# Second seven-product unit of the gate and up chunks moved from the sixth to the eighth plain slot

## The chip, the cores and the metric

The kernel runs on one NeuronCore of one Trainium2 chip. The metric is the device time of one execution in microseconds. An execution of the kernel before was also taken with the hardware profiler; the rows below come from that one.

## What is computed

The reference is one layer of a streaming encoder for 256 tokens of width 2048, all in float32. The change touches only its first and its last block, the two feed-forward networks (FFN), which have the same form:

```python
def _swiglu_ffn(x, norm_g, w_gate, w_up, w_down):
    h = _rmsnorm(x, norm_g)
    return (jax.nn.silu(h @ w_gate) * (h @ w_up)) @ w_down

h = h + 0.5 * _swiglu_ffn(h, ffn1_norm[l], ffn1_w_gate[l], ffn1_w_up[l], ffn1_w_down[l])
...
h = h + 0.5 * _swiglu_ffn(h, ffn2_norm[l], ffn2_w_gate[l], ffn2_w_up[l], ffn2_w_down[l])
```

`w_gate` and `w_up` are 2048 x 5632, `w_down` is 5632 x 2048. Between the two FFNs stand two recurrent branches, their merge and an attention over a memory; they are the same in both kernels.

## The kernel before, in words

**Split operands.** Every matrix product is made from three TensorE matmuls with 512 columns each: both operands are split into a high and a low part (`whi`, `wlo` for weights, `xhi`, `xlo` for activations), and the kernel adds high x high, low activation x high weight, high activation x low weight (lines 794 to 796). ScalarE makes the high part of a weight slot by a copy with rounding (line 371, function `split_hi`; line 847 inside a unit). VectorE makes the low part by subtraction (line 376, `split_lo`; line 865 inside a unit).

**Slots.** Weights come in raw slots of two 128 x 512 blocks (512 KB), loaded by the SP queue into a ring of four (`raw`); the split parts have a ring of four as well (`whi`, `wlo`). ScalarE may write slot n when TensorE has finished slot n - 4 (`slot_used`), VectorE when ScalarE has written it (`whi_ready`), TensorE reads it when VectorE has (`wlo_ready`), and SP loads a raw slot anew when VectorE has read it (`raw_free`).

**Gate and up chunks.** An FFN has 11 chunks of 512 hidden columns. Chunk 0 is made in the plain way. In chunks 1 to 10 (`SEVEN`) gate and up are made as a pair: six of the eight slots of gate and the same six of up are plain slots, t = 0 to 5 for gate and t = 6 to 11 for up (`na` is 6), with 12 matmuls each. The remaining slots 6 and 7 of both are two **units**: a unit takes one raw slot of gate and one of up and makes the eight block products of two token halves, two k blocks and gate or up from seven, with sums of weight blocks (VectorE, lines 872, 876 and 881, into `tw`), sums of activations (`xshi`, `xslo`) and sums of results. It fills four slots of the ring, `w` to `w + 3`, with 6, 6, 3 and 6 matmuls. Four of its results go into banks of their own (`pa`, `pb`), which both units of a chunk share. Where the units stand among the plain slots is written out in `GU_AFTER`: behind t = 1 and behind t = 5.

**What follows the second unit.** ScalarE copies one bank out (line 891, `copy_first`, at t = 6). VectorE combines the banks (lines 898 and 899, `combine`, at t = 8; line 902, `combine_last`, at t = 9) and adds the gate banks in (line 1063, at t = 9). Line 1063 releases the gate banks, for which TensorE waits at the start of the next chunk, and also frees ScalarE to apply the activation (line 982, at t = 10). The up half is subtracted, and gate times up is formed, in the next chunk, in the middle of its first unit (`gated`, lines 1025 and 1031, called between the second and third step of `unit_dve`). TensorE waits for that at the third slot of the unit.

**The hidden tile's way.** The result `hid` is turned by VectorE at t = 3 (line 705), written to DRAM and read back by the POOL queue (lines 668 and 678), then split at t = 9 by ScalarE (line 759, `hidden_hi`) and at t = 11 by VectorE (line 763, `hidden_lo`), which waits at line 1065 for the activation of its own chunk.

**What sets the order.** Each engine has its own loop over the same plain slots (`ffn_load` for SP, `ffn_pe`, `ffn_act`, `ffn_dve`), and what is to be done beside a slot is tied to its number t. The engines take their instructions in this order; semaphores alone tie them together. The chunk's last slot on one engine is followed at once by the next chunk's first.

Of the kernel before, what the change touches and what calls it, by code (L numbers as in the profile page):

```python
# [19 lines left out]
KT = D // P  # L20
# [5 lines left out]
NFC = F // CW  # L26
# [95 lines left out]


SEVEN = range(1, NFC)
GU_UNITS, GU_AFTER = (6, 7), (1, 5)
DN_UNITS = {"f1": ((0, 1, 2, 3, 4, 5), (2, 3, 4, 5)), "f2": ((0, 1, 2, 3, 4, 5), (0, 1, 2, 3, 4, 5))}
DN_AFTER = {"f1": ((7, 11, 15, 19, 23, 27), (5, 9, 13, 17)), "f2": ((7, 11, 15, 19, 23, 27), (3, 7, 11, 15, 19, 23))}
DN_FORMS = {5: 0, 9: 1, 17: 2}
# [3 lines left out]
def plan():  # L132

    prods, turns, nats = {}, {}, {}
    moved = {}
    state = dict(p=0, slot=0, raw=0, t=0, s=0, n=0, d=0, freed=[0, 0])
    raw_of, freed_by = {}, {}
    last = [None, None]

    def plain_slot():  # L140
        w, r = state["slot"], state["raw"]
        raw_of[w], freed_by[r] = r, w
        state["slot"] += 1
        state["raw"] += 1
        return w, r

    def unit_slots():

        w, r = state["slot"], state["raw"]
        freed_by[r], freed_by[r + 1] = w + 2, w + 2  # L150
        state["slot"] += UW
        state["raw"] += 2
        return w, r

    def pair_slots(a, b, units, after):

        js = [j for j in range(a["ns"]) if j not in units]
        pair = dict(a=a, b=b, after=after, plain=[], units=[], na=len(js))
        for t, (pr, j) in enumerate([(a, j) for j in js] + [(b, j) for j in js]):
            pair["plain"].append((pr, j, *plain_slot()))  # L160
            if t < len(js):
                a["done"] = state["slot"]
            if t in after:
                pair["units"].append((units[after.index(t)], *unit_slots()))
                a["done"] = state["slot"]
        b["done"] = state["slot"]
        a["pair"] = b["pair"] = pair

    def products(phase, n, nk, ups=None, seven=None):
        out = []  # L170
        for c in range(n):
            k = nk[c % len(nk)]
            par = state["p"] % 2
            if ups is not None and c % 2 == 1:
                released = ("nat_ready", ups + c // 2 + 1)
            else:
                state["freed"][par] += 1
                released = (("pair_free0", "pair_free1")[par], state["freed"][par])
            pr = dict(par=par, slot=state["slot"], raw=state["raw"], ns=k // SK, free=last[par], released=released)
            out.append(pr)  # L180
            last[par] = released
            state["p"] += 1
            if seven is not None and seven(c // 2) is not None:
                if c % 2 == 1:
                    pair_slots(out[-2], pr, *seven(c // 2))
                continue
            for j in range(pr["ns"]):
                plain_slot()
            pr["done"] = state["slot"]
        prods[phase] = out  # L190

    def turned(phase, n, split=True, nat=True, by_pe=None):
        by_pe = n if by_pe is None else by_pe
        turns[phase], nats[phase], moved[phase] = (state["t"] - (n - by_pe), state["s"]), state["n"], state["d"]
        state["t"] += by_pe
        state["d"] += n - by_pe
        if split:
            state["s"] += n
        if nat:
            state["n"] += n  # L200

    def ffn(tag):
        turned(tag + "norm", NDC, nat=False, by_pe=NDC if tag == "f1" else 1)
        turned(tag + "act", NFC, by_pe=0)
        products(tag + "gu", 2 * NFC, [KT], ups=nats[tag + "act"], seven=lambda i: (GU_UNITS, GU_AFTER) if i in SEVEN else None)
        products(tag + "dn", NDC, [FT], seven=lambda q: (DN_UNITS[tag][q], DN_AFTER[tag][q]))

    ffn("f1")
    turned("mixnorm", NDC, nat=False, by_pe=1)
    products("aux", 1, [KT])  # L210
    for hf in range(HALVES):
        products(f"gdn{hf}", 3, [KT])
    for hf in range(HALVES):
        products(f"rw{hf}", 3, [KT])
    products("gates", 2 * NDC, [KT])
    products("lift", 2 * NDC, [8])
    turned("merged", NDC, by_pe=1)
    products("out", NDC, [KT])
    turned("memnorm", NDC, by_pe=0)
    products("mkv", 2 * NDC, [KT])  # L220
    turned("mk", NDC, False, nat=False, by_pe=0)
    turned("qnorm", NDC, by_pe=0)
    products("mq", NDC, [KT])
    turned("mq", NDC, False)
    products("mo", NDC, [KT])
    ffn("f2")
    return prods, turns, nats, moved, raw_of, freed_by

# [27 lines left out]
def build(nc, A):  # L256

    prods, turns, nats, moved, raw_of, freed_by = plan()
    SUMS, ACTS, BANKS = count_marks()
    with ExitStack() as ctx:  # L260
        sems = {}

        def sem(name):
            if name not in sems:
                sems[name] = ctx.enter_context(nc.semaphore(name))
            return sems[name]
# [638 lines left out]
        def ffn_pe(pe, tag):  # L905
            gu, dn = prods[tag + "gu"], prods[tag + "dn"]
# [10 lines left out]
            for i in SEVEN:  # L917
                pair = gu[2 * i]["pair"]
                wait_pair(pe, pair["a"]["free"])
                for t in range(len(pair["plain"])):  # L920
                    plain_pe(pe, pair, t, (xhi, xlo))
                    if t in GU_AFTER:
                        n = GU_AFTER.index(t)
                        if n == 0:
                            pe.wait_ge(sem("banks_free"), BANKS[tag, "x"] if i == SEVEN[0] else BANKS[tag, "gu", i - 1])
                        unit_pe(pe, pair, n, (xhi, xlo), (xshi, xslo), n)
            pe.wait_ge(x_ready, s0 + NFC - 1)
            for q in range(NDC // 2):
                pair, after = dn[2 * q]["pair"], DN_AFTER[tag][q]
# [3 lines left out]
                for t in range(whole_slots):  # L933
# [3 lines left out]
                    if t in after:  # L937
                        n = after.index(t)
# [10 lines left out]
        def ffn_act(act, tag, then=None, gain=None):  # L949

            gu, dn = prods[tag + "gu"], prods[tag + "dn"]
# [15 lines left out]
            for i in SEVEN:  # L967
                pair = gu[2 * i]["pair"]
                gate = pair["a"]
                for t, (_, _, w, _) in enumerate(pair["plain"]):  # L970
                    split_hi(act, w, 0)
                    if t in GU_AFTER:
                        unit_act(act, pair, GU_AFTER.index(t), (tag, "gu", i))
                    if t == pair["na"]:
                        act.wait_ge(nat_ready, n0 + i)
                        copy_first(act, pair, cb[:, 0, :])
                    if t == pair["na"] + 3:
                        hidden_hi(act, tag, i - 1, hhi[:, 4 * i - 4:4 * i, :])
                    if t == pair["na"] + 4:
                        act.wait_ge(sem(gate["released"][0]), gate["released"][1])  # L980
                        for tt in range(TT):
                            op = nc.scalar.activation(gs[:, tt, :], cb[:, tt, :], ACT.Silu, scale=rstd[:, tt:tt + 1])
                        op.then_inc(sem("acts_ready"), 1)
            for q in range(NDC // 2):
                pair, after = dn[2 * q]["pair"], DN_AFTER[tag][q]
# [30 lines left out]
        def ffn_dve(dve, tag, then=None, gain=None):  # L1016
            gu, dn = prods[tag + "gu"], prods[tag + "dn"]
# [29 lines left out]
            for i in SEVEN:  # L1047
                pair = gu[2 * i]["pair"]
                gate = pair["a"]
                for t, (_, _, w, _) in enumerate(pair["plain"]):  # L1050
                    split_lo(dve, w, 0)
                    if t == 3:
                        nat_turn(dve, None, nats[tag + "act"] + i - 1)
                    if t in GU_AFTER:
                        n = GU_AFTER.index(t)
                        if n == 0 and i == SEVEN[0]:
                            dve.wait_ge(sem("banks_free"), BANKS[tag, "x"])
                        unit_dve(dve, pair, n, (tag, "gu", i), between=(lambda: gated(i - 1)) if n == 0 else None)
                    if t == pair["na"] + 2:
                        combine(dve, pair, cb, (tag, "gu", i))  # L1060
                    if t == pair["na"] + 3:
                        combine_last(dve, cb, (tag, "gu", i))
                        v.tensor_tensor(cb[:, 0:2, :], pair_of(gate), cb[:, 0:2, :], ALU.add).then_inc(sem(gate["released"][0]), 1)
                    if t == pair["na"] + 5:
                        dve.wait_ge(sem("acts_ready"), ACTS[tag, "gu", i, "gate"])
                        hidden_lo(dve, tag, i - 1, hhi[:, 4 * i - 4:4 * i, :], hlo[:, 4 * i - 4:4 * i, :])
            for q in range(NDC // 2):
                pair, after = dn[2 * q]["pair"], DN_AFTER[tag][q]
# [1923 lines left out]
```

## Time and profile before

| what | value |
|---|---|
| median of 3 runs | 2614.71 us (2613.63 to 2615.78) |
| the profiled execution, its own time | 2605.74 us |
| its span, first to last instruction | 2604.0 us |
| granted TensorE clock, mean | 0.998 |
| TensorE matmul busy | 2563.2 us (98%) |
| VectorE busy | 1954.3 us (75%) |
| ScalarE busy | 1341.0 us (51%) |

The span is what the rows below add up in; 1.74 us lie around it. A time in a row of the timeline is counted from the span's start. A matmul is shown with 0.39 us, but a new one starts every 0.2267 us, since they are pipelined: what counts is the distance of the starts. "[1.22 <-ACT whi L371]" behind a row says that the engine stood idle for 1.22 us before it and that ScalarE's line 371 ended this. In a wait row, "26.3, 10, 3.1" is the total in us, the number of times and the longest.

### The profile page before, as it was taken

Reading aid. Unit: us, or ns where it says so; the run is one execution under the profiler, and the core shown is the slowest. Engines: PE = TensorE matmul, PEld = TensorE weight load, DVE = VectorE, ACT = ScalarE, POOL = GpSimd, SP = SyncE. Lnnn points to the kernel's source line nnn. Section 1 sums busy time; section 2 is a strip of 40 time slices with the busy share of each in tenths; the row PEclk is TensorE's granted clock in tenths of the full one; section 3 lists DMA queues with packets and bytes.
Section 4 is the critical chain, followed back from the end, with each engine's and each line's share of the span. In section 5 each row is a group of like instructions: output and inputs, shape, how many; then the busy total and the mean of one; then the engine's idle time right before and its main releaser. Section 6 shows DMA issues by size and latency. Waiting matters only on the chain.

```text
span 2604.0 us, 34220 instructions
## 1 busy us (share of the span) xinstructions
PE 2563.2 (98%) x13659; PEld 2104.6 (81%) x13659; DVE 1954.3 (75%) x2311; ACT 1341.0 (51%) x1568; POOL 189.3 (7%) x346
## 2 busy tenths in 40 slices
PE   8999999998999999999999999999999999999998
PEld 7888888886788787878788888888888888888786
DVE  6888888876766796958666666555668888888876
ACT  5555555554456365546455444433455555555554
POOL 2000000000000011010001112000100000000000
PEclk9999999999999999999999999999999999999999
DMA  6767677666666675556488779644767676777554
GB/s 213 235 215 237 212 233 223 213 209 201 212 207 183 193 209 178 170 172 186 140 277 272 237 244 289 201 156 136 235 188 233 223 228 219 226 227 232 189 201 170
DMA packets 278576, 548.21 MB, mean 211 GB/s; under 512 B 25020, under 2 KB 35424, under 8 KB 278032
## 3 DMA queue, kind: packets, MB, share of 16 engines
q1 hardware_dynamic: 253904, 478.60, 58.3%
q0 software_dynamic: 24192, 66.89, 8.7%
q8 instruction: 107, 1.75, 0.3%
q10 hardware_dynamic: 320, 0.53, 0.1%
q14 instruction: 53, 0.43, 0.1%
HBM read 508.15 MB, written 37.77 MB: 210 GB/s over the span
## 4 chain that ended last, share of the span: by engine, by line
PE 68%; issue 18%; DVE 8%; DMA 3%; ACT 2%; POOL 1%; SPq 0%; DVEq 0%; ACTq 0%; POOLq 0%
PE pp L415 11%; PE pp L416 11%; PE pp L417 11%; PE pp L794 8%; PE pp L796 8%; PE pp L795 8%; DMA hid_dram<-hid_t 2%; DVE wlo L376 2%; POOL xq L678 1%; ACT whi L371 1%; PE pb L796 1%; PE pb L795 1%; PE pb L794 1%; PE pa L794 1%; PE pa L796 1%
## 5 line engine op out<-in xcount | busy, mean ns | idle before, releaser
L376 DVE TENSOR_TENSOR wlo<-raw,whi 128x1024 fp32r<-128x1024 f32 (+1 forms) x764 | 918.6, 1215 | 354.3 <-ACT whi L371 335.8
L371 ACT ACTIVATE whi<-raw 128x1024 fp32r<-128x1024 f32 (+1 forms) x764 | 798.7, 1054 | 620.6 <-PE pp L417 426.2
L794 PE MATMUL pp<-whi,xhi 128*128 128x512 f32 x1040 | 404.6, 389 | 0.0
L795 PE MATMUL pp<-whi,xlo 128*128 128x512 f32 x1040 | 404.6, 389 | 0.0
L796 PE MATMUL pp<-wlo,xhi 128*128 128x512 f32 x1040 | 404.6, 389 | 0.0
L415 PE MATMUL pp<-whi,xhi 128*128 128x512 f32 (+1 forms) x928 | 370.3, 399 | 0.7 <-DVE xlo L533 0.7
L417 PE MATMUL pp<-wlo,xhi 128*128 128x512 f32 (+1 forms) x928 | 359.3, 387 | 0.0
L416 PE MATMUL pp<-whi,xlo 128*128 128x512 f32 (+1 forms) x928 | 359.2, 387 | 0.0
L847 ACT ACTIVATE whi<-tw 128x1024 fp32r<-128x1024 f32 x124 | 131.6, 1062 | 272.4 <-PE pp L796 122.9
L794 PE MATMUL pp<-whi,hhi 128*128 128x512 f32 x572 | 224.6, 393 | 14.4 <-DVE wlo L376 14.4
L795 PEld LDWEIGHTS pp<-whi,xlo 128*128 128x128 f32 x1040 | 195.2, 188 | 40.7
L796 PEld LDWEIGHTS pp<-wlo,xhi 128*128 128x128 f32 x1040 | 195.2, 188 | 40.5
L794 PEld LDWEIGHTS pp<-whi,xhi 128*128 128x128 f32 x1040 | 195.2, 188 | 40.3
L795 PE MATMUL pp<-whi,hlo 128*128 128x512 f32 x572 | 223.3, 390 | 0.0
L796 PE MATMUL pp<-wlo,hhi 128*128 128x512 f32 x572 | 223.1, 390 | 0.0
L415 PEld LDWEIGHTS pp<-whi,xhi 128*128 128x128 f32 x928 | 174.4, 188 | 43.2 <-issue 7.2
L417 PEld LDWEIGHTS pp<-wlo,xhi 128*128 128x128 f32 x928 | 174.3, 188 | 36.1
L865 DVE TENSOR_TENSOR wlo<-tw,whi 128x1024 fp32r<-128x1024 f32 x124 | 151.5, 1222 | 67.6 <-ACT whi L847 67.6
L416 PEld LDWEIGHTS pp<-whi,xlo 128*128 128x128 f32 x928 | 174.6, 188 | 32.3
L847 ACT ACTIVATE whi<-raw 128x1024 fp32r<-128x1024 f32 x124 | 104.7, 845 | 121.9 <-PE pp L796 89.4
L794 PEld LDWEIGHTS pp<-whi,hhi 128*128 128x128 f32 x572 | 107.7, 188 | 40.9 <-DVE wlo L376 18.6
L872 DVE TENSOR_TENSOR tw<-raw 128x1024 f32<-128x1024 f32 x62 | 75.9, 1225 | 79.2 <-DMA raw<-in_ffn_w_up 48.4
(528 smaller groups left out, 3670.3 us busy)
## 6 DMA issues: line engine op xcount, KB each, us to landing
raw<-in_ffn_w_gate SPq DMA_DIRECT2D x176, 512.0 KB, 4.4
raw<-in_ffn_w_up SPq DMA_DIRECT2D x176, 512.0 KB, 4.6
raw<-in_ffn_w_down SPq DMA_DIRECT2D x176, 512.0 KB, 4.6
raw<-in_w_in SPq DMA_DIRECT2D x144, 512.0 KB, 4.4
hid_dram<-hid_t POOLq DMA_DIRECT2D x43, 512.0 KB, 4.9
xq<-hid_dram POOLq DMA_DIRECT2D x156, 128.0 KB, 4.0
raw<-in_w_lift SPq DMA_DIRECT2D x32, 512.0 KB, 5.5
raw<-in_w_out SPq DMA_DIRECT2D x32, 512.0 KB, 5.3
```

Source lines behind the costliest of these rows:

```text
L371: nc.scalar.activation(whi[:, s, :, 0:width], raw[:, r % RING, :, 0:width], ACT.Copy).then_inc(whi_ready, 1)
L376: nc.vector.tensor_tensor(wlo[:, s, :, 0:width], raw[:, r % RING, :, 0:width], whi[:, s, :, 0:width].bitcast(F32), ALU.subtract).then_inc( ...
L415: nc.tensor.matmul(out, a_hi[:, k0 + k, tok], w_hi, start=first, stop=False)
L416: nc.tensor.matmul(out, a_lo[:, k0 + k, tok], w_hi, start=False, stop=False)
L417: mm = nc.tensor.matmul(out, a_hi[:, k0 + k, tok], w_lo, start=False, stop=final)
L678: nc.gpsimd.dma_start(landing[rows, :, :, :].rearrange("p q m j -> p q (m j)"), scratch.rearrange("(q i) e -> i q e", q=4)[:, :, 256 * b:2 ...
L794: nc.tensor.matmul(out, a_hi, whi[:, s, block, :], start=start, stop=False)
L795: nc.tensor.matmul(out, a_lo, whi[:, s, block, :], start=False, stop=False)
L796: return nc.tensor.matmul(out, a_hi, wlo[:, s, block, :], start=False, stop=stop)
L847: nc.scalar.activation(dst, src, ACT.Copy).then_inc(whi_ready, 1)
L865: v.tensor_tensor(dst, src, hi.bitcast(F32), ALU.subtract).then_inc(wlo_ready, 1)
L872: v.tensor_tensor(tw[:, 0:2, :], blocks[:, b11:b22 + 1:3, :], blocks[:, b12:b12 + 1, :].to_broadcast([P, 2, CW]), ALU.add).then_inc(sem("s ...
```

## The change

In chunks 1 to 9 of both FFNs the second unit stands behind t = 7, two slots into up, instead of behind t = 5. Chunk 10 keeps its places. What follows the unit is now tied to the unit's place instead of to `na`: the copy comes at t = 8, the combination at t = 10, its last step and line 1063 at t = 11, and the activation at t = 11, the chunk's last slot. `hidden_hi` and `hidden_lo` keep t = 9 and t = 11; the wait ahead of `hidden_lo` is left in chunk 10 only. The loads follow the same lists, so the two raw slots of the second unit are loaded two places later.

```diff
-GU_UNITS, GU_AFTER = (6, 7), (1, 5)
+GU_UNITS = (6, 7)
+GU_AFTER = {i: (1, 7) if i < NFC - 1 else (1, 5) for i in SEVEN}
...
-        products(tag + "gu", 2 * NFC, [KT], ups=nats[tag + "act"], seven=lambda i: (GU_UNITS, GU_AFTER) if i in SEVEN else None)
+        products(tag + "gu", 2 * NFC, [KT], ups=nats[tag + "act"], seven=lambda i: (GU_UNITS, GU_AFTER[i]) if i in SEVEN else None)
...
-                    if t in GU_AFTER:
-                        n = GU_AFTER.index(t)
+                    if t in pair["after"]:
+                        n = pair["after"].index(t)
...
-                    if t == pair["na"]:
+                    if t == pair["after"][-1] + 1:
                         act.wait_ge(nat_ready, n0 + i)
                         copy_first(act, pair, cb[:, 0, :])
                     if t == pair["na"] + 3:
                         hidden_hi(act, tag, i - 1, hhi[:, 4 * i - 4:4 * i, :])
-                    if t == pair["na"] + 4:
+                    if t == min(pair["after"][-1] + 5, len(pair["plain"]) - 1):
                         act.wait_ge(sem(gate["released"][0]), gate["released"][1])
...
-                    if t == pair["na"] + 2:
+                    if t == pair["after"][-1] + 3:
                         combine(dve, pair, cb, (tag, "gu", i))
-                    if t == pair["na"] + 3:
+                    if t == pair["after"][-1] + 4:
                         combine_last(dve, cb, (tag, "gu", i))
                         v.tensor_tensor(cb[:, 0:2, :], pair_of(gate), cb[:, 0:2, :], ALU.add).then_inc(sem(gate["released"][0]), 1)
                     if t == pair["na"] + 5:
-                        dve.wait_ge(sem("acts_ready"), ACTS[tag, "gu", i, "gate"])
+                        if i == NFC - 1:
+                            dve.wait_ge(sem("acts_ready"), ACTS[tag, "gu", i, "gate"])
                         hidden_lo(dve, tag, i - 1, hhi[:, 4 * i - 4:4 * i, :], hlo[:, 4 * i - 4:4 * i, :])
```

The third hunk stands three times, once for each of the three engines' loops.

## Rows read from the trace of the kernel before

**Rows 1.** The page: busy time, share of the span and instructions of each engine.
```profile
PE 2563.2 (98%) x13659; PEld 2104.6 (81%) x13659; DVE 1954.3 (75%) x2311; ACT 1341.0 (51%) x1568; POOL 189.3 (7%) x346
```
**Rows 2.** Windows, chunks 1 to 10: length; PE, PEld, DVE, ACT, POOL busy; clock; DMA.
```profile
57.50:479.00 421.50, 421.50 (x1861) 349.04 (x1860) 354.31 (x348) 226.91 (x241) 27.60 (x50) 1.00 0.72 224
1936.50:2358.20 421.70, 421.70 (x1862) 349.28 (x1861) 354.67 (x348) 227.15 (x241) 27.54 (x50) 1.00 0.71 224
```
**Rows 3.** Timeline of TensorE, chunk 4 to chunk 5: start us, us, instruction.
```profile
190.97 0.39 PE L794 MATMUL pa<-whi,xhi 128*128 128x512 f32 x1
...
211.37 0.39 PE L794 MATMUL pp<-whi,xhi 128*128 128x512 f32 x1
...
233.13 0.39 PE L794 MATMUL pa<-whi,xhi 128*128 128x512 f32 x1
```
**Rows 4.** Timeline of ScalarE, end of chunk 4, from behind its second unit.
```profile
209.67 2.05 ACT L371 ACTIVATE whi<-raw 128x1024 fp32r<-128x1024 f32 x2
211.96 1.06 ACT L371 ACTIVATE whi<-raw 128x1024 fp32r<-128x1024 f32 x1 [0.23 <-DMA raw<-in_ffn_w_up]
212.93 1.04 ACT L759 ACTIVATE hhi<-xq 128x1024 fp32r<-128x1024 f32 x1
...
218.13 1.34 ACT L982 ACTIVATE gs<-cb,rstd 128x512 f32<-128x512 f32 x2 [2.72 <-DVE cb L1063]
219.37 2.00 ACT L371 ACTIVATE whi<-raw 128x1024 fp32r<-128x1024 f32 x2
```
**Rows 5.** Timeline of VectorE over the same stretch.
```profile
210.76 2.36 DVE L376 TENSOR_TENSOR wlo<-raw,whi 128x1024 fp32r<-128x1024 f32 x2 [0.20 <-ACT whi L371]
...
215.01 1.23 DVE L376 TENSOR_TENSOR wlo<-raw,whi 128x1024 fp32r<-128x1024 f32 x1
...
216.87 1.23 DVE L1063 TENSOR_TENSOR cb<-pp,cb 128x1024 f32<-128x1024 f32 x1
...
220.45 1.23 DVE L376 TENSOR_TENSOR wlo<-raw,whi 128x1024 fp32r<-128x1024 f32 x1 [1.22 <-ACT whi L371]
```
**Rows 6.** Timeline of VectorE over the first unit of chunk 4.
```profile
183.18 1.23 DVE L872 TENSOR_TENSOR tw<-raw 128x1024 f32<-128x1024 f32 x1 [0.26 <-DMA raw<-in_ffn_w_up]
...
188.64 1.22 DVE L865 TENSOR_TENSOR wlo<-tw,whi 128x1024 fp32r<-128x1024 f32 x1
189.78 0.69 DVE L881 TENSOR_TENSOR tw<-tw,raw 128x512 f32<-128x512 f32 x1
...
192.32 1.23 DVE L865 TENSOR_TENSOR wlo<-tw,whi 128x1024 fp32r<-128x1024 f32 x1 [1.26 <-ACT whi L847]
```
**Rows 7.** Timeline of ScalarE, the high part of that unit's last slot.
```profile
191.23 1.06 ACT L847 ACTIVATE whi<-tw 128x1024 fp32r<-128x1024 f32 x1 [2.08 <-PE pp L796]
```
**Rows 8.** Timelines of VectorE and TensorE in the down products, a short hold.
```profile
2467.42 1.22 DVE L376 TENSOR_TENSOR wlo<-raw,whi 128x1024 fp32r<-128x1024 f32 x1
...
2468.70 0.50 PE L794 MATMUL pp<-whi,hhi 128*128 128x512 f32 x1 [1.30 <-DVE wlo L376]
...
2470.90 0.40 PE L794 MATMUL pp<-whi,hhi 128*128 128x512 f32 x1
```
**Rows 9.** Window 57.5 to 479: a wait, and landing times of DMAs (last number, us).
```profile
ACT gs L982 <- DVE cb L1063: 26.3, 10, 3.1
...
raw<-in_ffn_w_up SPq DMA_DIRECT2D x79, 512.0 KB, 4.7
...
xq<-hid_dram POOLq DMA_DIRECT2D x40, 128.0 KB, 3.2
```
**Rows 10.** Timeline of POOL in chunk 4, the hidden tile's way.
```profile
203.09 2.19 POOL L678 DMA_DIRECT2D xq<-hid_dram  x4 [4.81 <-DMA hid_dram<-hid_t]
```
**Rows 11.** TensorE around the longest hold: timeline, and a window (columns as in rows 2).
```profile
613.86 0.80 PE L794 MATMUL pp<-whi,hhi 128*128 128x512 f32 x1 [6.73 <-DVE wlo L376]
...
616.15 0.63 PE L796 MATMUL pp<-wlo,hhi 128*128 128x512 f32 x1
...
613.00:625.00 12.00, 11.14 (x42) 9.10 (x43) 11.57 (x19) 6.19 (x10) 0.56 (x1) 0.83 0.54 175
```

More of the change, by code:

```diff
@@ L971, in ffn_act @@
                     split_hi(act, w, 0)
-                    if t in GU_AFTER:
-                        unit_act(act, pair, GU_AFTER.index(t), (tag, "gu", i))
-                    if t == pair["na"]:
+                    if t in pair["after"]:
+                        unit_act(act, pair, pair["after"].index(t), (tag, "gu", i))
+                    if t == pair["after"][-1] + 1:
                         act.wait_ge(nat_ready, n0 + i)
@@ L1053, in ffn_dve @@
                         nat_turn(dve, None, nats[tag + "act"] + i - 1)
-                    if t in GU_AFTER:
-                        n = GU_AFTER.index(t)
+                    if t in pair["after"]:
+                        n = pair["after"].index(t)
                         if n == 0 and i == SEVEN[0]:
```

## The prediction

> **What bounds the kernel now.** I read the page first: TensorE is busy in 2563.2 us, 98% of the span [rows 1]. Its eleven chunks of gate and up products per FFN are the only part that the change touches, so the second view is the table of two windows over chunks 1 to 10 of each FFN. TensorE is busy in 421.50 of 421.50 us and in 421.70 of 421.70, at granted clock 1.00, which is the 2.4 GHz level; VectorE is busy in 354 of them, ScalarE in 227 [rows 2]. Third, the timeline of TensorE in chunk 4: the first product of the first unit (unit 6; the second is unit 7) starts at 190.97 and the same product of chunk 5 at 233.13, so a chunk takes 42.16 us. It has 12 plain slots of 12 products and two units of 21, 186 in all, which gives 0.2267 us a product, and the 96 products from 211.37 to 233.13 have the same pitch [rows 3]. Nothing stands between them: TensorE alone sets the length of these chunks. A reordering of the same 186 products can win nothing there; it can only use up the lead that VectorE has over TensorE. The whole question is how much of it is left.
>
> In units of this pitch a plain slot takes 2.72 us and a unit 4.76. The four slots of a unit have 6, 6, 3 and 6 products, so its last starts 15 products, 3.40 us, after its first. VectorE needs about 1.14 us for the low part of a full slot wherever it stands, so it gains on TensorE over plain slots and loses over units.
>
> **The change, part by part.** No instruction is added or removed on any engine and no byte is moved more; one wait is dropped. The second unit moves from behind slot t = 5 to behind t = 7, in chunks 1 to 9 of both FFNs. Behind it there were six plain slots (16.32 us) and there are now four (10.88 us). The work that must follow the unit (combination, release of the gate banks, activation) does not shrink with them.
>
> Step 1, when the gate banks are released. Before, the unit ends at 211.37, where the next plain product starts [rows 3], and the addition of line 1063, which releases them, ends at 216.87 + 1.23 = 218.10 [rows 5], 6.73 us later. The order on VectorE is the same after the change (three low parts, two combination steps, a low part, the last step, line 1063). On ScalarE one thing differs: the conversion of the hidden tile (line 759) is tied to t = 9, which used to be the fourth slot behind the unit and is now the second. So it stands ahead of the third high part. That one followed at 209.67 + 0.99 = 210.66 before [rows 4]; with steps of 0.97 and 0.94 as at 211.96, 212.93 and on, it starts at 209.67 + 0.97 + 0.94 = 211.58 and ends at 212.64. The low part that waits for it then ends at 212.67 + 1.23 = 213.90 instead of 210.76 + 2.36 = 213.12: 0.78 later. Release comes 6.73 + 0.78 = 7.51 us after the unit, 10.88 - 7.51 = 3.37 us ahead of the next chunk. Before it was 9.59 ahead. TensorE itself, which waits for this release, is still not held.
>
> Step 2, what is behind that release. The activation (line 982) waits for it, and moves from t = 10 to t = 11, the chunk's last place on ScalarE. Behind it in ScalarE's queue stand the high parts of the next chunk. Before, ScalarE stood 2.72 us in this wait [rows 4], which two further high parts made good. Now from release to the end of the next high part is 219.37 + 1.06 - 218.10 = 2.33 us (the first of the pair in rows 4), and to the end of its low part 221.68 - 218.10 = 3.58 [rows 5]. That is 0.21 us after the chunk's end.
>
> Step 3, VectorE's row of work that follows. The low part of t = 1 starts at 3.49 after release and takes 1.14; then unit 6 begins, with the gating of the chunk before in its middle. From its first sum to the end of the low part of its second slot is 183.18 to 189.86, 6.68 us; to the end of the sum of line 881 it is 190.47 - 183.18 = 7.29 [rows 6]. So that sum ends at 3.49 + 1.14 + 7.29 = 11.92 after release. ScalarE's high part of the last slot waits for it: 0.04 + 1.06 [rows 7], then the low part 0.03 + 1.23 [rows 6]: 14.28. TensorE, unheld, would be there at 3.37 + 5.44 (two slots) + 3.40 = 12.21. It comes 2.07 us late. What a hold costs beside the lateness is seen once in the down products: the low part ends at 2468.64, the product starts at 2468.70, and the nine products from there take 2.20 us where nine pitches are 2.04 [rows 8]. That is 0.06 + 0.16. I take **2.07 + 0.06 + 0.16, rounded, 2.28 us a chunk**. The holds before this one (the chunk's first slot, the unit's second) are part of it, not added: the last slot's time is fixed by VectorE.
>
> Step 4, does it grow? The high part of the next plain slot follows 0.95 behind, its low part ends at about 15.4, and TensorE wants it at 12.21 + 2.28 + 1.36 = 15.85. From there VectorE wins 1.5 us a slot again, and before unit 7 there are now six slots for it. So each chunk starts from the same state, and the loss is paid once for each of the chunks 2 to 10: 9 x 2 x 2.28 = **41.0 us**.
>
> Step 5, what I cost at nothing. The wait of line 1065 ahead of the hidden tile's low part is dropped; TensorE never saw it, being busy throughout [rows 2], so nothing is won. The loads on SP keep their number; unit 7's two come two places later, and the next unit's second is issued 1.86 us ahead of release, lands by a median of 4.7 later [rows 9] and is wanted at 4.63: 1.8 us of cover. Gone, it costs what it is late. On POOL, the four reads of the hidden tile start at 203.09 over 2.19 us [rows 10]; they land some 3.2 after their issue [rows 9], by 208.5, and are wanted at 209.67 + 0.97 = 210.6. The turn (line 705) shifts by about as much as TensorE does. Unit 6 in TensorE waits for line 902, done 9 us ahead.
>
> Sum against the profiled execution: 2605.74 + 41.0 = 2646.7. The median of the three runs is 2614.71, 9 us above that execution; I add the same sum to it: **2655.7 us**.
>
> Bounds. Below: nothing for the restart (-0.16) and nothing for the conversion that moves ahead (-0.78) leave 1.34 us, 24 us in all. Above: a restart paid at each of three holds (+0.32) and 0.1 of slack give 2.7, 49 us. The row values lie between, and I take them since each is from the same stage. With 1.5 us for the runs' own spread and 2 more for what is left out, the range is 2637 to 2667.
>
> **Rivals.** (a) Only the chunk's first slot is late: VectorE finds room in unit 6. Then each chunk pays 0.21 + 0.06 + 0.16 = 0.43, 8 us in all, 2622. For it: at unit 6's second slot there are 2.5 us to give today (low part done at 189.86, wanted at 190.97 + 1.36 = 192.33). Against: its last slot is ready at 193.55 and wanted at 190.97 + 3.40 = 194.37 [rows 3, 6]; 0.8 is to give there, and VectorE comes 2.07 + 0.82 = 2.9 later against TensorE. (b) Not slower: the place is again the row of work from line 1063 to unit 6's last slot. It decides at 12.21 us; if the row is 2.07 shorter than I add it up, nothing is held and the time stays at 2614.7. The activation would have to run without keeping the next high parts waiting. Against it is ScalarE's order, which has the activation first, and its 26.3 us of waits for line 1063 in ten chunks [rows 9]. A gain would have to come from the 9 us by which the runs exceed the profiled execution; if those were late loads in these chunks, up to 9 us could go. (c) Worse than forecast: three short holds in 10 us bring the clock down. After a hold of 6.73 us the five products from 613.86 to 616.15 take 0.46 us each instead of 0.227, and the granted clock is 0.83 over the 12 us from 613, between full and the level of 1.2 GHz. That is some 2 us lost [rows 11]; eighteen times it is 37 more, 2693. Against: after 1.30 us of idle nine products took 0.24 each, the full level [rows 8].
> The Trainium skill, page "TensorE: Matmul & The Clock Gate", section "A second HAM failure mode: psum-queue depth-cycling", says that frequent very short idles between groups of matmuls can make the clock swing between half and full; by that rule (c) would be the outcome, and the short hold of this trace does not bear it out.
>
> **Chances.** The forecast with its bounds 0.80; (a) and what lies between it and 2637 0.07; (b) 0.06, of which 0.02 for a gain; (c) or late loads, above 2667, 0.07. What a measurement here can tell from no change is 0.2%, 5.2 us. So faster 0.02, same 0.04, slower 0.94.
>
> **What would show it.** In the profile after: TensorE idle in the gate and up windows, about 2 us a chunk, in chunks 2 to 10 and not in 1; released by the low part of unit 6's second and last slots, and slightly at the chunk's first; chunks 44.4 us apart; line 1063 ending 7.5 us behind the unit; DVE waiting on ScalarE's high part at the chunk's start. If the chunks are still 42.16 apart, steps 2 and 3 are wrong; if only the first slot is held, step 3; if the pitch rises to 0.4, (c) is right.

## The result

| | median | runs | range |
|---|---|---|---|
| kernel before | 2614.17 us | 4 | 2613.12 to 2615.78 |
| changed kernel | 2651.31 us | 4 | 2648.69 to 2652.74 |

The ratio is 1.014, with a 95% interval of 1.0123 to 1.0158: 37.1 us slower (32 to 41). The forecast was 2655.7 us in a range of 2637 to 2667, that is 41.0 us slower than the 2614.71 us that it started from. The range holds the result; the forecast is 4.4 us above the measured median, and its loss is 3.9 us above the measured one. The profiled execution of the changed kernel took 2652.68 us with a span of 2650.9.

Windows of the changed kernel over the chunks of the first line in [rows 2]. Chunk 1 fills the first window, the nine chunks behind it the second; the third is one chunk's start. Line numbers of the changed kernel are one higher than before from line 125 on, and two higher in the last part.

```profile
core 0: us, PE busy (x) PEld busy (x) DVE busy (x) ACT busy (x) POOL busy (x), PEclk, DMA share, GB/s
57.50:102.00 44.50, 44.50 (x197) 36.64 (x196) 33.05 (x33) 22.46 (x25) 2.82 (x5) 1.00 0.65 202
102.00:504.00 402.00, 388.41 (x1679) 312.80 (x1679) 324.24 (x318) 200.58 (x218) 24.67 (x45) 1.00 0.68 214
...
191.00:203.00 12.00, 10.69 (x45) 8.25 (x46) 11.44 (x13) 5.14 (x6) 0.00 (x0) 1.00 0.45 133
```

TensorE, which had no idle time in these chunks, still has none in chunk 1, and stands idle for 13.6 us in the nine chunks behind it. The timeline of TensorE, as in [rows 3], shows where; the lines below give the first product of the first unit in two chunks that follow each other, and every product ahead of which TensorE stood idle.

```profile
191.11 0.47 PE L795 MATMUL pp<-whi,xhi 128*128 128x512 f32 x1 [0.21 <-DVE wlo L377]
196.64 0.39 PE L795 MATMUL pa<-whi,xhi 128*128 128x512 f32 x1
198.74 0.50 PE L795 MATMUL pb<-whi,xshi 128*128 128x512 f32 x1 [0.59 <-DVE wlo L866]
201.70 0.50 PE L795 MATMUL pa<-whi,xshi 128*128 128x512 f32 x1 [0.61 <-DVE wlo L866]
...
235.48 0.47 PE L795 MATMUL pp<-whi,xhi 128*128 128x512 f32 x1 [0.16 <-DVE wlo L377]
241.04 0.39 PE L795 MATMUL pa<-whi,xhi 128*128 128x512 f32 x1
```

The chunk takes 241.04 - 196.64 = 44.40 us instead of 42.16. TensorE is held (kept waiting for an operand) three times: at the chunk's first slot, at the second slot of the first unit and at its last, each time by a low part. Idle time understates a hold, since a row's modelled end is later than the next start: measured from start to start, the three add up to the 2.24 us.

VectorE over the same chunk end and start, to set beside [rows 5, 6]:

```profile
179.24 1.23 DVE L377 TENSOR_TENSOR wlo<-raw,whi 128x1024 fp32r<-128x1024 f32 x1 [0.21 <-ACT whi L372]
181.18 1.23 DVE L377 TENSOR_TENSOR wlo<-raw,whi 128x1024 fp32r<-128x1024 f32 x1 [0.71 <-ACT whi L372]
...
186.16 1.23 DVE L1064 TENSOR_TENSOR cb<-pp,cb 128x1024 f32<-128x1024 f32 x1
187.30 1.21 DVE L764 TENSOR_TENSOR hlo<-xq,hhi 128x1024 fp32r<-128x1024 f32 x1
189.74 2.36 DVE L377 TENSOR_TENSOR wlo<-raw,whi 128x1024 fp32r<-128x1024 f32 x2 [1.22 <-ACT whi L372]
192.01 1.22 DVE L873 TENSOR_TENSOR tw<-raw 128x1024 f32<-128x1024 f32 x1
...
194.88 1.22 DVE L1026 TENSOR_TENSOR cb<-pp,cb 128x1024 f32<-128x1024 f32 x1
196.14 1.42 DVE L1032 SCALAR_TENSOR_TENSOR hid<-cb,rstd,gs 128x512 f32<-128x512 f32 x2
197.47 1.22 DVE L866 TENSOR_TENSOR wlo<-tw,whi 128x1024 fp32r<-128x1024 f32 x1
198.60 0.69 DVE L882 TENSOR_TENSOR tw<-tw,raw 128x512 f32<-128x512 f32 x1
...
200.42 1.23 DVE L866 TENSOR_TENSOR wlo<-tw,whi 128x1024 fp32r<-128x1024 f32 x1 [0.52 <-ACT whi L848]
```

And ScalarE, to set beside [rows 4]: the hidden tile's conversion now stands ahead of the third high part, and the activation waits 4.94 us, not 2.72, with the next chunk's high parts queued behind it.

```profile
179.11 1.05 ACT L760 ACTIVATE hhi<-xq 128x1024 fp32r<-128x1024 f32 x1
180.09 1.06 ACT L372 ACTIVATE whi<-raw 128x1024 fp32r<-128x1024 f32 x1
...
187.42 1.34 ACT L983 ACTIVATE gs<-cb,rstd 128x512 f32<-128x512 f32 x2 [4.94 <-DVE cb L1064]
188.66 1.99 ACT L372 ACTIVATE whi<-raw 128x1024 fp32r<-128x1024 f32 x2
```

Read against the release of the gate banks (line 1064 ends at 187.39): VectorE idles 1.22 us until the first high part behind the activation is there, the first low part (the first of the two in the row at 189.74) ends at 190.96, the sum of line 882 at 199.29 and the last slot's low part at 201.65. TensorE starts that slot at 201.70.

### The profile page after: what moved, and what is told of

It is laid out like the page before. It is cut to its first block, busy times and chain, and to the rows that moved or that the text cites. A ratio compares the mean times of both kernels' runs of the same rounds, so it can differ in the third digit from the quotient of the medians.

```text
span 2650.9 us, 34202 instructions
## 1 busy us (share of the span) xinstructions
PE 2582.8 (97%) x13659; PEld 2103.6 (79%) x13659; DVE 1956.6 (74%) x2311; ACT 1330.1 (50%) x1568; POOL 188.6 (7%) x346
## 4 chain that ended last, share of the span: by engine, by line
PE 56%; issue 22%; DVE 13%; ACT 4%; DMA 4%; POOL 1%; SPq 0%; DVEq 0%; ACTq 0%; POOLq 0%
PE pp L416 10%; PE pp L418 10%; PE pp L417 10%; PE pp L795 6%; PE pp L797 6%; PE pp L796 6%; DVE wlo L377 3%; DMA hid_dram<-hid_t 3%; ACT whi L372 2%; POOL xq L679 1%; DVE wlo L866 1%; PE pa L795 1%; PE pb L2385 1%; PE pa L2400 1%; DVE hid L1032 0%
```

## The experiments

The theory is the forecast's: from release to the first unit's last slot VectorE and ScalarE have a fixed row of work, and four plain slots behind the second unit are too few to hide it. Rival L: the second unit's loads, which now come later, hold TensorE. Rival O: the activation's place as the last thing of the chunk on ScalarE is the whole cause. Rival V: VectorE has too much to do in a chunk, wherever it does it. Ratios are to the kernel before on the same chip (2611.5 us median in both sets), and the differences in us are worked out from them and from that median. The plain difference of the medians is 2 to 3 us larger for the conversion's and the activation's move (31.9 and 16.9 us), and about 1 us off at most elsewhere. The steady distance of two chunks, read as above, tells more than the total, since single late loads add to the latter.

### The second unit one slot earlier

```diff
-GU_AFTER = {i: (1, 7) if i < NFC - 1 else (1, 5) for i in SEVEN}
+GU_AFTER = {i: (1, 6) if i < NFC - 1 else (1, 5) for i in SEVEN}
```

> The second unit stands behind t = 6 in place of t = 7 in chunks 1 to 9, and what follows it one slot earlier; the activation stays at t = 11. Theory (the tail behind the unit is too short for VectorE's row of work): release comes 6.73 us behind the unit, since the hidden tile's conversion is again behind the third high part, so 13.60 - 6.73 = 6.87 us ahead of the next chunk; the last slot of the first unit is wanted 6.87 + 8.84 = 15.71 us after release and its low part is done at 14.26, so no hold, chunks 42.16 us apart, 2614 us as before. Rival L (the later places of the second unit's loads hold TensorE): about half of the loss stays, some 18 us. Rival O (any place past t = 5 costs the same, through the activation at t = 11 that keeps ScalarE from the next high parts): the full 37 us stay.

Measured: ratio 1.0007 (0.9996 to 1.0017), no difference. Timeline of TensorE, the first unit's first product in two chunks; there is no held product between them:

```profile
191.54 0.39 PE L795 MATMUL pa<-whi,xhi 128*128 128x512 f32 x1
...
233.71 0.39 PE L795 MATMUL pa<-whi,xhi 128*128 128x512 f32 x1
```

The distance is 42.17 us. The activation is the last of the chunk on ScalarE here too, so rival O in its strong form falls, and half of the loads' shift costs nothing in the steady pattern (one chunk of the second FFN takes 43.39 us, held at its first unit's last slot). Between no loss and 37 us lies one slot of 2.72 us.

### The hidden tile's conversion one slot later

```diff
-                    if t == pair["na"] + 3:
+                    if t == (pair["after"][-1] + 3 if i < NFC - 1 else pair["na"] + 3):
                         hidden_hi(act, tag, i - 1, hhi[:, 4 * i - 4:4 * i, :])
```

> The changed kernel, with the high part of the hidden tile taken behind the third high part after the second unit (t = 10) instead of the second (t = 9). Theory: release comes 0.78 us earlier, the first unit's last slot is late by 2.07 - 0.78 = 1.29, with 0.22 for the hold 1.51 us a chunk in place of 2.23, 18 x 1.51 = 27 us over the kernel before: 2641 us. Rival L (loads): nothing changes, 2651. Rival O (the activation's place alone): nothing changes, 2651.

Measured: ratio 1.0113 (1.0094 to 1.0132), 29.5 us over before, 24.5 to 34.5. TensorE:

```profile
194.50 0.39 PE L795 MATMUL pa<-whi,xhi 128*128 128x512 f32 x1
196.27 0.49 PE L795 MATMUL pb<-whi,xshi 128*128 128x512 f32 x1 [0.25 <-DVE wlo L866]
199.22 0.50 PE L795 MATMUL pa<-whi,xshi 128*128 128x512 f32 x1 [0.62 <-DVE wlo L866]
...
238.11 0.39 PE L795 MATMUL pa<-whi,xhi 128*128 128x512 f32 x1
```

The hold at the chunk's first slot is gone and the chunk takes 43.61, so 1.45 us are lost where 1.51 were expected, 26 us in eighteen chunks. The 0.78 us of step 1 are real. Rivals L and O expected no change.

### The activation behind the next chunk's first two high parts

```diff
+                    late = gate if t == pair["na"] + 4 and i == NFC - 1 else gu[2 * i - 2] if t == 1 and i > 1 else None
+                    if late is not None:
+                        act.wait_ge(sem(late["released"][0]), late["released"][1])
...
                     if t in pair["after"]:
                         unit_act(act, pair, pair["after"].index(t), (tag, "gu", i))
...
-                    if t == min(pair["after"][-1] + 5, len(pair["plain"]) - 1):
-                        act.wait_ge(sem(gate["released"][0]), gate["released"][1])
...
```

> The changed kernel, with the activation of chunks 1 to 9 taken in the next chunk behind ScalarE's high part of t = 1, ahead of the first unit. Theory: the next chunk's first two high parts no longer wait for release; VectorE goes from line 1064 through the hidden tile's low part to the low parts of t = 0 and 1 without idle, which brings the first sum of the unit from 4.63 to about 3.30 us after release. The unit's last slot is then 0.74 late, 0.96 us a chunk with the hold, 17 us over the kernel before: 2631 us; the hold at the chunk's first slot and at the unit's second are gone. Rival L (loads): 2651 unchanged. Rival O (the activation alone): all of the loss is gone, 2614.

Measured: ratio 1.0052 (1.0033 to 1.0071), 13.6 us over before, 9 to 19. TensorE:

```profile
193.08 0.39 PE L795 MATMUL pa<-whi,xhi 128*128 128x512 f32 x1
197.25 0.50 PE L795 MATMUL pa<-whi,xshi 128*128 128x512 f32 x1 [0.59 <-DVE wlo L866]
...
236.15 0.39 PE L795 MATMUL pa<-whi,xhi 128*128 128x512 f32 x1
```

The activation itself, left out of the lines above, moves with its wait. A chunk takes 43.07 us: 0.91 lost where 0.96 were expected, 16 us in eighteen chunks, and one hold of the three is left, at the unit's last slot. Rival O expected none, rival L all three.

### Both edits together

The diffs are the two above.

> Both of the edits before, in one kernel; the second unit stays behind t = 7 and the loads keep the changed order. Theory: they add up, the unit's last slot is done at 12.93 us after release and wanted at 12.97, so a hold of at most 0.2 us a chunk is left: 2614 to 2618 us. Rival L (loads): 2651. Rival O: 2614, as with the activation's move alone.

Measured: ratio 1.0026 (1.0015 to 1.0037), 6.8 us over before, 3.9 to 9.7. TensorE:

```profile
191.06 0.39 PE L795 MATMUL pa<-whi,xhi 128*128 128x512 f32 x1
...
233.36 0.39 PE L795 MATMUL pa<-whi,xhi 128*128 128x512 f32 x1
```

42.30 us a chunk, 0.14 lost (expected at most 0.2), which is some 2.5 us in all. The order of the loads is that of the changed kernel, so rival L falls as the cause of the steady loss. The total is above the expected 0 to 4 us: in the profile three chunks take 0.7 to 0.9 us longer than the others. What that is stands at the end.

### One more VectorE instruction, in the changed kernel and in the repaired one

```diff
                     if t == pair["na"] + 5:
...
+                        if i < NFC - 2:
+                            dve.wait_ge(hi_ready, s0 + i)
+                            nc.vector.tensor_tensor(by_token(hlo[:, 4 * i:4 * i + 4, :]), hidden, by_token(hhi[:, 4 * i - 4:4 * i, :]).bitcast(F32), ALU.subtract)
                         hidden_lo(dve, tag, i - 1, hhi[:, 4 * i - 4:4 * i, :], hlo[:, 4 * i - 4:4 * i, :])
```

> The changed kernel with one more VectorE instruction of 1.22 us (the hidden tile's low part once more, into a place that the next chunk writes over) at t = 11, behind line 1064, in chunks 1 to 8 of both FFNs. Theory: VectorE stands 1.22 us idle there for ScalarE's next high part, which is held by the activation, so the instruction falls into idle time: hold and chunk (44.4 us) stay, 2651 us. Rival V (it is VectorE's work per chunk that is too much, wherever it stands): 16 x 1.14 = 18 us more, 2669.

> The same instruction in the same place, added to the kernel with both repairs, in which VectorE runs from line 1064 to the first unit without idle. Theory: now it stands in the row of work, the first unit's last slot is 1.14 us later and nearly all of this is held: chunks of 43.45 instead of 42.31 us, 16 x 1.14 = 18 us more than that kernel. Rival V: the same 18 us as in the run beside it, not 0 there. Rival N (a margin is left in the repaired kernel): under 8 us.

Measured: 1.0167 (1.0152 to 1.0182) for the first, 1.0082 (1.0066 to 1.0097) for the second. VectorE in the first, the added instruction being line 1070:

```profile
186.15 1.23 DVE L1064 TENSOR_TENSOR cb<-pp,cb 128x1024 f32<-128x1024 f32 x1
187.29 1.22 DVE L1070 TENSOR_TENSOR hlo<-xq,hhi 128x1024 fp32r<-128x1024 f32 x1
188.42 1.22 DVE L764 TENSOR_TENSOR hlo<-xq,hhi 128x1024 fp32r<-128x1024 f32 x1
189.74 2.36 DVE L377 TENSOR_TENSOR wlo<-raw,whi 128x1024 fp32r<-128x1024 f32 x2
```

The low parts start at 189.74, to the hundredth where they started in the changed kernel; only the idle 1.22 us ahead of them are filled. The first unit begins at 196.65 and 241.05 in the two chunks, a distance of 44.40 as without the instruction. In the repaired kernel the same two rows of TensorE read

```profile
193.98 0.39 PE L795 MATMUL pa<-whi,xhi 128*128 128x512 f32 x1
198.53 0.50 PE L795 MATMUL pa<-whi,xshi 128*128 128x512 f32 x1 [0.62 <-DVE wlo L866]
...
237.42 0.39 PE L795 MATMUL pa<-whi,xhi 128*128 128x512 f32 x1
```

43.44 instead of 42.30: the instruction costs 1.14 us a chunk there, its whole start-to-start length. The same work is free in one kernel and paid in full in the other, so rival V falls. The totals follow less neatly. The first is 43.6 us over before (39.7 to 47.5) where the changed kernel was 32 to 41, with chunks of the same length; the second is 14.6 us over the repaired kernel's 6.8 where 18 were expected.

### Without the subtraction of the up half

```diff
                 if i in SEVEN:
-                    link(dve, v.tensor_tensor(cb[:, 2:4, :], pair_of(up), cb[:, 2:4, :], ALU.subtract))
                     dve.wait_ge(sem("acts_ready"), ACTS[tag, "gu", i, "gate"])
```

> The changed kernel without the subtraction of the up half (line 1026), which opens the gating work in the middle of the first unit; this part of the computation is left out. Theory: VectorE's row from release to the unit's last slot is 24.14 - 22.88 = 1.26 us shorter, the hold 2.23 - 1.26 = 0.97 us a chunk, 18 x 1.26 = 23 us less than the changed kernel, some 2629 us. Rival O (the hold is fixed by the activation at t = 11 alone, at the chunk's first slot): no change, 2651, since the first slot's hold does not depend on line 1026.

Measured: ratio 1.0074 (1.0061 to 1.0088), 19.3 us over before where 18 were expected. TensorE:

```profile
194.38 0.39 PE L795 MATMUL pa<-whi,xhi 128*128 128x512 f32 x1
198.19 0.50 PE L795 MATMUL pa<-whi,xshi 128*128 128x512 f32 x1 [0.24 <-DVE wlo L866]
...
237.53 0.39 PE L795 MATMUL pa<-whi,xhi 128*128 128x512 f32 x1
```

The distance of 43.15 is 1.25 less than the changed kernel's 44.40, for 1.26 expected. The gating work in the middle of the first unit is part of the row that sets the loss, one for one; rival O expected no change. The hold at the chunk's first slot is still there and has become part of the rest.

### The same thing in the down products, on top of the kernel before

If a hold comes from what VectorE or ScalarE wait for ahead of the split parts, then the holds that the kernel before has in its down products [rows 8, 11] should go by moving those waits. This kernel has the gate and up chunks of before.

```diff
-DN_TURNS = (0, 2, 4, 12, 14)
+DN_TURNS = (0, 5, 7, 14, 16)
...
-                    if q == 1 and t == after[-1] + 4:
+                    if q == 1 and t == after[-1] + 6:
                         down_sumsq(act, tag, 2)
...
+                    if q == 1 and t == 0 and then is not None:
+                        h_turn(dve, then, 0, dn[0])
...
-                    if t == after[-1] + 1:
+                    if t == after[-1] + 2:
                         combine(dve, pair, tw, mark)
                         combine_last(dve, tw, mark)
-                    if t == after[-1] + 2:
+                    if t == after[-1] + 3:
                         down_add(dve, c0 + 1, tw[:, 2:4, :], -0.5)
+                    if t == after[-1] + 4:
                         down_add(dve, c0, tw[:, 0:2, :], 0.5)
-                    if t == after[-1] + 3:
                         residual(dve, dn[c0], c0, 0.5)
-                    if t == after[-1] + 4 and then is not None:
+                    if q == 1 and t == after[-1] + 5 and then is not None:
                         h_turn(dve, then, c0, dn[c0])
```

> The kernel before, with VectorE's in-line waits of the down products put where its lead is large: combination behind the second, not the first, slot after the last unit and the additions spread over two slots more, and the turned tile of the next norm taken at t = 5 in place of t = 2 of the second pair. Theory (a hold of TensorE comes from what VectorE or ScalarE wait for ahead of the split parts): four holds of 1.47 + 0.77 + 0.2 us in the down products and one of 6.9 + 1.6 us go, 10 + 8 = 18 us less than before, 0.7%. Rival W (the held work returns as a later hold, at the next unit or at the norm behind the FFN): under 5 us.

Measured: 2593.64 us against 2611.52, ratio 0.9935 (0.9922 to 0.9947): 17 us faster, 14 to 20. Windows over the down products of the two FFNs, first in the kernel before, then in this one:

```profile
480.00:727.00 247.00, 236.45 (x1031) 193.81 (x1030) 184.84 (x205) 120.00 (x138) 11.01 (x20) 0.99 0.62 202
2359.00:2597.00 238.00, 233.77 (x1025) 191.57 (x1023) 187.54 (x193) 119.79 (x132) 3.31 (x6) 1.00 0.59 196
```

```profile
482.00:716.00 234.00, 233.52 (x1030) 192.70 (x1029) 184.17 (x204) 119.91 (x139) 10.97 (x20) 1.00 0.66 212
2351.00:2585.00 234.00, 232.77 (x1024) 191.44 (x1022) 187.18 (x193) 119.59 (x132) 3.30 (x6) 1.00 0.59 199
```

The idle time of TensorE falls from 10.55 to 0.48 us in the first and from 4.23 to 1.23 us in the second, with the same products done. The windows are 13 and 4 us shorter: 13.1 us of this is idle time and the other 3.9 us busy time, of which some 2 us are the products behind the long hold, with the granted clock of 0.83 over 12 us [rows 11]. The 18 us expected lie in the interval, and rival W, by which the holds come back elsewhere, falls. The long hold of [rows 11] is down to two short ones of 0.26 and 0.22 us of idle time. This version beats both kernels; it was timed as a whole, and which part of the gain belongs to which of its two edits was not timed apart.

## Why the prediction was right

**Step 1** (release 7.51 us behind the second unit, 3.37 ahead of the next chunk). In the trace after, the unit ends at 179.86, where the first plain product behind it starts, and release comes at 187.39: 7.53 behind it and 3.35 ahead of the chunk's unheld end. The 0.78 us in it were confirmed by moving the hidden tile's conversion.

**Step 2** (the activation keeps the next high parts; first low part 3.58 us after release). 190.96 - 187.39 = 3.57.

**Step 3** (11.92 us to the sum, 14.28 to the last low part, 2.07 late, 2.28 with the hold). 11.90, 14.26, and a steady loss of 2.24 us. The run without line 1026 and the one with the instruction added show from both sides that this row, and nothing beside it, sets the loss.

**Step 4** (paid once for each of chunks 2 to 10). Chunk 1 has no hold, and the distances from first unit to first unit do not grow. The first of each FFN is 42.6 us, since only the hold at chunk 2's first slot lies in it; of the sixteen others fourteen lie between 44.33 and 44.44 us. Counted by chunks, it is 18 x 2.24 = 40.3 us.

**Step 5** (loads, the POOL queue and the dropped wait at nothing). It held for the steady loss. It left out single late loads, and it looked only at the loads of the next chunk's first unit: those of the moved unit are waited for in every chunk, as the last section tells, and in the profile of the changed kernel two chunks are longer by it.

**The sum** was 41.0 us, the medians show 37.1 (32 to 41), the two profiled executions 46.9. The last figure is made of about 40 us of steady loss, 1.9 in two chunks with late loads (distances of 44.87 and 45.79), 0.8 ahead of the first unit of the first FFN, and some 4.4 from the second unit of that FFN's last chunk to the first unit of the second FFN; the change touches neither of the last two stretches (the latter takes 1484.06 us before and 1488.43 after; the other runs with the moved unit show 1486 to 1496 there). Why the medians lie 3 us below the steady loss isn't settled; their interval covers it.

**The rivals.** (a), only the first slot held, falls by the three holds. (b), not slower, falls: the row took 14.26 us, and not 2.07 less. Its condition, an activation that keeps no high part waiting, was made by an edit; alone it left 0.91 us a chunk, together with the conversion's move 0.14. (c), a falling clock, falls by the window from 191 to 203 us, which has all three holds and a granted clock of 1.00, the 2.4 GHz level. The Trainium skill's rule of short idles that make the clock swing (page "TensorE: Matmul & The Clock Gate", section "A second HAM failure mode: psum-queue depth-cycling") was not borne out here, with three idles of 1.4 us in all in a chunk of 44.4.

## What to carry to other kernels

When the engine that bounds a stage has no idle time, a reordering can only spend the lead of those that feed it. Write down when the last result ahead of a boundary is released, and add up the in-order work from there to the tightest slot behind it. In these traces a wait at a chunk's end (4.94 us ahead of the activation) delayed everything behind it on the same engine, so put an instruction that waits behind the work that the bounding engine needs next, or at a place where the lead is long. The same instruction cost nothing a chunk in one kernel and its full length, 1.14 us, in the other: what decided was whether its engine had idle time ahead of the next thing that the path needed.

## What the runs showed of the hardware that was not expected

Single loads landed far later than the median. Over the gate and up chunks of the first FFN the landing times of the 512 KB loads, as minimum, median and maximum, are in the kernel before, and behind it in the changed one:

```profile
DMA to landing us min/median/max: 3.4/4.5/8.7
```

```profile
DMA to landing us min/median/max: 3.5/4.7/10.8
```

The kernel before took loads of 8.7 us in its stride, with all its chunks at 42.16 us. With the lead spent, a late load becomes a hold: in the changed kernel, ScalarE waited for one 4.26 us in the chunk whose distance is 45.79.

```profile
392.42 1.06 ACT L848 ACTIVATE whi<-raw 128x1024 fp32r<-128x1024 f32 x1 [4.26 <-DMA raw<-in_ffn_w_gate]
```

The kernel with both repairs has the same in single chunks (43.05, 43.18 and 43.21 us beside 42.30), which is 2.5 of the 4 us by which its total exceeds its steady loss. In the chunk ahead of each of the three, and in no other of chunks 1 to 9, ScalarE's third high part behind the second unit waited for its load, 0.73 to 0.81 us, and the release came later with it:

```profile
259.47 1.06 ACT L372 ACTIVATE whi<-raw 128x1024 fp32r<-128x1024 f32 x1 [0.77 <-DMA raw<-in_ffn_w_up]
```

So a lead that the steady pattern doesn't need is still worth something against single late loads. The waits go with the order of the loads. Over the gate and up chunks of one FFN, ScalarE and VectorE waited 40 to 45 us for loads in the two kernels with the second unit behind t = 5 (before, and the one with changed down products), 67 to 69 us with it behind t = 6, and 70 to 82 us in the seven kernels with it behind t = 7; the longest landing was 8.4 to 9.0 us, 8.4 to 8.8 us and 8.9 to 10.8 us. How the order brings this about was not tried.
